# Norm sums, token scales and high parts between dense stages, attention by head pairs, and expert outputs by feature

## The reference, cut to what matters

```python
def rms(x):
    return x * lax.rsqrt(jnp.mean(x * x, axis=-1, keepdims=True) + EPS)

def modulate(h, shift, scale):
    return h * (1 + scale) + shift

def layer(x, xc, ...):                       # x and xc go through the same steps
    x = x + 0.5 * g1 * swiglu(modulate(rms(x), sh1, sc1), pre_wi, pre_wo)
    x = x + g2 * mixer(modulate(rms(x), sh2, sc2), ...)
    x = x + 0.5 * g3 * swiglu(modulate(rms(x), sh3, sc3), post_wi, post_wo)

def window_gqa(...):                         # 16 query heads, 4 key heads, head width 64
    # scores of 128 queries over 256 latent and 256 context keys, masked beyond 128 tokens
    p = jax.nn.softmax(jnp.concatenate([s_w, s_c, sink_b], axis=-1), axis=-1)
    o = p_w @ v_w + p_c @ v_c

def peer_ffn(z, wq, subkeys, u_tab, v_tab):  # 8 heads x 16 experts for each token
    # expert, gate: the 16 best of 16 x 16 sums of two sub-key scores, and their softmax
    h = jnp.einsum('thkd,td->thk', u_tab[expert], zb)
    act = gate * jax.nn.gelu(h, approximate=False)
    return jnp.einsum('thk,thkd->td', act, v_tab[expert])
```

## Time and profile before

| | us |
|---|---|
| median of three executions | 4268.56 |
| lowest, highest | 4261.12, 4279.62 |
| the profiled execution | 4257.62 |
| its span, first to last instruction | 4255.8 |
| granted TensorE clock, mean | 0.978 of 2.4 GHz |

### The profile page before, as it was taken

How to read it: one execution, slowest core, us unless ns; L and a number is a source line. 1 busy time by engine, 2 the same in 40 slices (tenths; PEclk the granted TensorE clock), 3 DMA queues, 4 the chain that set the end, 5 groups by cost and what they waited for, 6 DMA issues and landing times. The chain is left out here.

```text
span 4255.8 us, 50533 instructions
## 1 busy us (share of the span) xinstructions
PE 3832.7 (90%) x17626; PEld 2701.9 (63%) x17626; DVE 2633.9 (62%) x5211; ACT 1667.1 (39%) x3644; POOL 624.1 (15%) x665
## 2 busy tenths in 40 slices
PE   6999988999999999998999888788789998887877
PEld 4788765788788865897878744233278787442322
DVE  6877556677565546656347666777553466677774
ACT  3222535323332245543225444444332254444443
POOL 1100000000000000000000143444300002444442
PEclk9999998999999999999999999999999999999999
DMA  5554111355333310553033599999920346999997
GB/s 213 202 184 173 70 40 55 119 181 171 128 141 131 125 61 1 199 186 120 11 129 129 220 420 420 420 420 420 375 80 21 129 146 248 420 420 420 420 420 310
DMA packets 135007, 904.29 MB, mean 212 GB/s; under 512 B 14855, under 2 KB 15879, under 8 KB 35168
## 3 DMA queue, kind: packets, MB, share of 16 engines
q0 software_dynamic: 95552, 620.97, 36.2%
q1 hardware_dynamic: 39200, 280.08, 18.5%
HBM read 899.90 MB, written 5.28 MB: 213 GB/s over the span
## 5 line engine op out<-in xcount | busy, mean ns | idle before, releaser
L2511 PE MATMUL ps<-arena 128*128 128x512 f32 x1640 | 809.8, 622 | 183.1 <-ACT arena L2574 181.5
L2670 DVE CUSTOM_DVE_ANT_0 arena<-arena 128x1024 f32<-128x1024 f32 x410 | 502.5, 1226 | 326.6 <-DMA arena<-peer_uv,arena 325.5
L620 DVE TENSOR_TENSOR w_lo<-wt,w_hi 128x1024 fp32r<-128x1024 f32 x388 | 475.4, 1225 | 351.7 <-ACT w_hi L602 328.1
L2511 PEld LDWEIGHTS ps<-arena 128*128 128x128 f32 x1640 | 292.4, 193 | 628.4 <-ACT arena L2574 402.0
L655 PE MATMUL ps<-h_hi,w_hi 128*128 128x512 f32 (+1 forms) x1744 | 649.4, 372 | 32.5 <-DVE h_lo L742 22.5
L2642 POOL DMA_INDIRECT arena<-peer_uv,arena x410 | 433.4, 1057 | 1583.3 <-DVEq L2633 989.2
L602 ACT ACTIVATE w_hi<-wt 128x1024 fp32r<-128x1024 f32 x388 | 407.6, 1058 | 636.1 <-PE ps L655 607.0
L655 PE MATMUL ps<-h_lo,w_hi 128*128 128x512 f32 (+1 forms) x1744 | 639.5, 367 | 0.0
L655 PE MATMUL ps<-h_hi,w_lo 128*128 128x512 f32 (+1 forms) x1744 | 639.2, 367 | 0.0
L450 PE MATMUL ps<-hT,wt 128*128 128x256 f32 x1632 | 407.0, 387 | 6.1 <-ACT hT L1389 5.1
L655 PEld LDWEIGHTS ps<-h_hi,w_hi 128*128 128x128 f32 x1744 | 332.1, 190 | 94.0 <-issue 17.7
(11 more groups left out here) (342 smaller groups left out, 5453.8 us busy)
## 6 DMA issues: line engine op xcount, KB each, us to landing
wt<-wstream SPq DMA_DIRECT2D x262, 1024.0 KB, 4.9
ada_t<-adastream POOLq DMA_DIRECT2D x133, 512.0 KB, 3.7
arena<-peer_uv,arena POOLq DMA_INDIRECT x410, 20.3
arena<-adastream POOLq DMA_DIRECT2D x11, 512.0 KB, 26.6
bias_by_query<-bias_by_distance POOLq DMA_DIRECT2D x1, 4096.0 KB, 17.3
arena<-bias_by_query POOLq DMA_DIRECT2D x1, 3072.0 KB, 12.1
xT<-tokens SPq DMA_DIRECT2D x1, 2048.0 KB, 15.2
cst<-consts SPq DMA_DIRECT2D x1, 1816.0 KB, 9.0
```

The source lines that it names most:

```text
L620: self.step(self.dve.tensor_tensor(lo, raw_group(g), hi.bitcast(F32), ALU.subtract))
L2511: ins = pe.matmul(bank, diag[n % DIAGS], row[:, at:at + 512], start=s == 0, stop=s == SLOTS - 1)
L2670: dve.tensor_tensor_reduce(u, u, ztok[:, t], 1.0, 0.0, ALU.mult, ALU.add, hbuf[:, t, s:s + 1]).then_inc(dot_ready.sem, 1)
```

## The change

1. **Norm sums by column.** `dve_part` adds into `rstd` (or, in `merge`, into the slot it used before) instead of `hT[:, 0]`, so that the squares' slots come free one by one. Residual m of a last pass now stands behind sum m-1, and not before it.
2. **Scale kept in the tokens.** Behind sum m-1 DVE writes `xT` times the next norm's scale into `hT` (`dve_scaled`, 2 instructions of 256 tokens for a chunk), for chunks 0 to 6; chunk 7 is done in the norm. The norm then multiplies `hT` by `rstd`.
3. **High parts written directly and used first.** ACT adds the shift and writes `h_hi` in one step (2 instructions instead of 3); DVE makes `h_lo` from `hT`, shift and `h_hi` (2 instead of 1). `pe_by_chunk` starts a chunk when `h_hi` is there: hi x hi and lo x hi for all columns, then waits for `h_lo` and adds hi x lo for all. The first FFN keeps its own norm but uses the new order on PE.
4. **`keep_on`** leaves the start of dense stages: 4 such products now stand right behind `pe_parts`, and in `b_out` they wait for one bank instead of four.
5. **Plain norms** (`ln1`, `lnf`): DVE multiplies by gain and `rstd` in one step; ACT's step is gone.
6. **Head pairs.** `b_attend` has 16 units of two heads: scores of two heads in two halves of the rows, 1024-wide maxima and copies, value products of the two heads alternating between column halves, two pairs of score banks and one pair of transpose banks.
7. **Experts by feature.** A slot makes eight products of 128 columns: a block of 128 features of the row is the stationary operand, `diag` the moving one, and the result has features on partitions. ACT's copies and PE's transposes at the end go.

```diff
-        def pe_parts(pe, mm, T):
+        def pe_parts(pe, mm, T, idle=0):
             pe.wait_ge(A_.free, A_.given_back())
             bank = A_.claim()
             pe.wait_ge(sum_ready.sem, sum_ready.due(pe))
-            mm(bank[:, 0:T], ones, hT[:, 0, 0:T], True, False)
+            mm(bank[:, 0:T], ones, rstd[:, 0:T], True, False)
             pe.wait_ge(part_ready.sem, part_ready.due(pe, DC))
             mm(bank[:, 0:T], ones, hT[:, DC - 1, 0:T], False, True, A_.full)
+            if idle:
+                pe.wait_ge(D_.free, D_.given_back())
+                keep_on(pe, D_.coming(), idle)
...
+            if last and m >= 2:
+                dve_part(dve, step, m - 1, T)
+            if last and nxt and m >= 2:
+                for k in (0, 1) if m == 2 else (m - 1,):
+                    dve_scaled(dve, step, k, T, *nxt)
+            dve.wait_ge(D_.full, D_.filled())
+            bank = D_.take()
...
+        def pe_by_chunk(pe, SW, columns, T, key):
+            for k in range(DC):
+                pe.wait_ge(h_hi_ready.sem, h_hi_ready.due(pe))
+                ws = []
+                for c, r, bank in columns:
+                    hi, lo = SW.next(*key(k, c))
+                    ws.append(hi)
+                    SW.mm(bank[:, 0:T], ((hi, h_hi[:, k, 0:T]), (lo, h_hi[:, k, 0:T])), k == 0, False, None)
+                pe.wait_ge(h_ready.sem, h_ready.due(pe))
+                for hi, (c, r, bank) in zip(ws, columns):
+                    SW.mm(bank[:, 0:T], ((hi, h_lo[:, k, 0:T]),), False, k == DC - 1, r.full if k == DC - 1 else None)
...
+                    for x in range(2):
+                        mm(s[:, x, :], qB[r, u, q * P:(q + 1) * P], kD[r, u // 2, :], True, False)
+                    for x in range(2):
+                        mm(s[:, x, far], ident, const("window", q, TOK)[:, far], False, True, SB.scored if x else None)
...
+                        for x in range(2):
+                            mm(o[x * HD:(x + 1) * HD, 0:P], vB[:, j, g * HD:(g + 1) * HD], t[:, x, j, :], j == 0, j == 3,
+                               SB.valued if j == 3 and x else None)
...
-                    for bank, at in zip(y_banks(t), (D, D + 512)):
-                        ins = pe.matmul(bank, diag[n % DIAGS], row[:, at:at + 512], start=s == 0, stop=s == SLOTS - 1)
+                    for m in range(DC):
+                        ins = pe.matmul(y_banks(t)[m // 4][:, (m % 4) * P:(m % 4 + 1) * P], row[:, D + m * P:D + (m + 1) * P],
+                                        diag[n % DIAGS], start=s == 0 and m % 4 == 0, stop=s == SLOTS - 1,
+                                        skip_group_check=True)
```

More of the change, by code:

```diff
@@ L523, in act_squares, with dve_norm @@
             act_parts(act, step, T)
[L525 to L530, removed]
+        def dve_norm(dve, T, gain, first):
             dve.wait_ge(rstd_ready.sem, rstd_ready.due(dve))
             for k in range(DC):
[L533 to L539, removed]
+                dve.scalar_tensor_tensor(out=hT[:, k, 0:T], in0=xT[:, k, 0:T], scalar=v(gain, first + k),
+                                         in1=rstd[:, 0:T], op0=ALU.mult, op1=ALU.mult).then_inc(h_ready.sem, 1)
         def modulate(act, l, which, T, k):
@@ L654, in mm @@
                 for i, (a, b) in enumerate(pairs):
[L655 removed]
+                    ins = self.pe.matmul(o, a, b, start=start and i == 0, stop=stop and i == len(pairs) - 1)
                 if inc is not None:
@@ L675, in h_parts, with pe_split_project @@
             return h_hi[:, k, t0:t1], h_lo[:, k, t0:t1]
-        def pe_split_project(pe, SW, name, cols, T, r, abreast=0, idle=0):
+        def pe_by_chunk(pe, SW, columns, T, key):
[9 more added lines that the diff above has]
+                    SW.mm(bank[:, 0:T], ((hi, h_lo[:, k, 0:T]),), False, k == DC - 1, r.full if k == DC - 1 else None)
+        def pe_split_project(pe, SW, name, cols, T, r, abreast=0):
             if abreast:
                 pe.wait_ge(r.free, r.given_back(abreast))
[L681 to L687, removed]
+                pe_by_chunk(pe, SW, [(c, r, r.claim()) for c in cols[:abreast]], T, lambda k, c: (name, 0, k * P, c))
             for c in cols[abreast:]:
@@ L808, in pe_ffn @@
                 pe.wait_ge(r.free, r.given_back(ABREAST))
-            abreast = [(half, j, r, r.claim()) for j in range(ABREAST) for half, r in ((0, A_), (1, D_))]
-            if not first:
-                keep_on(pe, abreast[-1][3], 7 if T == TOK else 5)
-            for k in range(DC):
-                pe.wait_ge(h_ready.sem, h_ready.due(pe))
-                for half, j, r, bank in abreast:
-                    w = SW.next(f"ffn_{which}_wi", l, k * P, half * FF + j * P)
-                    SW.mm(bank[:, 0:T], three(w, h_parts(k, 0, T)), k == 0, k == DC - 1,
-                          r.full if k == DC - 1 else None)
+            abreast = [(half * FF + j * P, r, r.claim()) for j in range(ABREAST) for half, r in ((0, A_), (1, D_))]
+            pe_by_chunk(pe, SW, abreast, T, lambda k, c: (f"ffn_{which}_wi", l, k * P, c))
             for part in range(0, FC, HALF):
@@ L1217, in dve_a_out @@
                 weights.ahead()
-                dve.wait_ge(D_.full, D_.filled())
-                dve_residual(dve, step, D_.take(), m, 0, 1, TOK, True)
+                dve_residual(dve, step, m, 0, 1, TOK, True, (0, 2))
         MB = Carve(SPLIT_END)
```

233 lines of the change are left out of this document (120 added, 113 removed).

## The result

| | before | after |
|---|---|---|
| median, us | 4267.68 (4 runs) | 4228.09 (4 runs) |
| lowest, highest | 4261.12, 4279.62 | 4219.72, 4229.76 |
| span of the profiled execution | 4255.8 | 4217.9 |

The ratio is 0.9899, with a 95% interval from 0.9877 to 0.9921: 39.6 us off the median, where 56 were forecast (4212). The time lies in the forecast range, which was 43 us wide. Measured again beside three experiments the same kernel gave 4232.63 us (6 runs), ratio 0.9904 (0.9881 to 0.9928).

A forecast was written before the change was run, and what follows sets the result against it. Gathers bound `peer`; PE bounds `b_attend` and the dense stages, with losses between these. Terms summed to -56 us: profiled 4257.6 to 4201.6, plus 11 for the median, 4212 us; eight-in-ten range 4190 to 4233.

The forecast's parts named there:

- the signs that the prediction set itself: Profile checks: first products 6.5 us behind the last stage, `b_attend` near 62 us; wrong if passages are still 9 us.
- Head pairs, -33: `b_attend`: 16 pairs at 3.62 us plus 4 us of filling make 62 us against 94.8.
- The rival that DVE takes the stage: `b_attend`: DVE sets the pace at 4.2 us a pair, +9 us, 4221 us in all; chance 0.14.
- `a_out` to `post 0`, -5.2: Dense passage: same sequence as `post 0` to `pre 1`, with no blocks or weights beside it on DVE; 5.2 us less.
- `post 0` to `pre 1`, -4.9: Dense passage: earlier sums and `rstd`, first product near 1131.3 instead of 1136.4; residual 7 late by up to 0.2 us.
- the 1 us forecast for the first norm: First norm: high products of chunk 6 run before PE's wait for its low part; -1 us, from 0 to -3.5.
- `b_out` to `post 1`, +0.7: 256-token passage: DVE's late scalings cost +3.8, earlier sums and fewer constants give back; +0.7 us, between -1.5 and +3.
- `pre 0` to `a_qkv` and `pre 1` to `b_qkv`: Passages with their blocks: earlier `rstd` gives 1.65 and 1.25 us, the norm's pace 1.85 each; -3.5 and -3.1 together.
- Plain norms, -2.6: ACT's step leaves the way: -1.6 us at the first `rwkv_in`, -0.7 at the second, -0.3 at the final norm.
- Experts by feature, -3.6: `peer`: slots stay below the gathers' pace; each of two stages ends 1.8 us earlier, -3.6 us.
- rival (c): `peer`: loads and products don't overlap, PE becomes the bound at 4.5 us a slot; +970 us, 5180 us; chance 0.03.
- Rival (b): Four dense passages: late residual 7 or a falling clock shrinks their 16.7 us gain to 6; 4222 us; chance 0.11.

The follow-up runs named there:

- the two best versions: Changed kernel with last chunk column by column, later scaling in `a_out`, `b_out` and for chunk 6: 4212.47 us; also without constants behind `pre 1` and `b_out`: 4198.03 us.

## Why the prediction came out as it did

The time came into the range, but not for the reasons given. The pairs came as worked out. The dense stages, forecast to give 17 us, gave next to nothing in all, and the range was wide enough to hold that. By the signs that the prediction set itself, one passage is wrong: counted as there, from the end of the last product, first products stand 7.5 to 8.8 us behind in three of the four passages of 512 tokens, where 6.5 was forecast, and 10.1 us behind in `a_out` to `post 0`, where 9 was called wrong. PE was busy 94.9% of `b_attend` (over 95% forecast) and DVE idle 0.73 us a pair (under 0.4), so DVE was further from the bound than I had it.

- **Head pairs, -33: right, -31.6.** Every term of a pair was read from rows of the kernel before, most of them of other stages, and stood within 0.02 us. The filling was 63.2 - 16 x 3.59 = 5.8 us instead of 4; 0.8 of it is the stretch at 1.2 GHz, the other 1 us is open. The rival that DVE takes the stage is out: DVE is busy 72% of it. The section PSUM Bottleneck of the Trainium skill's page "TensorEngine Tiling (Array Packing)" warns of this bound; in this stage it wasn't met. The pairs also left `b_out` 1.7 us longer, at a clock of 0.91 (the run with pairs alone), which wasn't forecast.
- **`a_out` to `post 0`, -5.2: wrong step, -1.2.** I wrote that DVE has "no blocks or weights beside it". It splits weights for each chunk there, 1.23 us. Four of the eight banks come full together, 22.5 us before the last product ends; the seven steps from residual 0 to residual 7, 4.09 us each in the middle, take 26.0 us. Without the added scalings the passage is 6.66 us: -5.0, nearly the size forecast. Its sums also ran partly at 1.2 GHz behind the longer waits (the row of 2.07 us above), which came in with the late residual.
- **`post 0` to `pre 1`, -4.9: right mechanism, -3.8.** The residual was 1.3 us late and not 0.2.
- **Abreast block: not in the sum, +8.1 in three bodies and +1.5 in `a_out` and `b_out`.** I looked at when PE may begin a chunk, and not at when a bank is full, for which `silu` and the next weight split wait. This term was missing in `post 0`, `pre 1` and `post 1`, and ate the 1 us forecast for the first norm as well.
- **`b_out` to `post 1`, +0.7: +1.6, and the body +0.6.** DVE's lateness was forecast. The constants were counted at -1.3; in truth they stand ahead of the stage's end for all engines, and the passage is 2.9 us shorter without them. The same at `pre 1` to `b_qkv` is 1.9 us.
- **`pre 0` to `a_qkv` and `pre 1` to `b_qkv`: -3.6 and -2.7, with nothing from their blocks.** The sums of about -3.5 and -3.1 came out, the split of them didn't: the passages alone were to give 1.65 and 1.25 us. In `pre 0` to `a_qkv` the sums behind the shorter wait ran at 2.4 GHz (1.10 and 1.13 us for the halves). This is luck in part: in three of the nine profiles with parts 1 to 3 the clock fell to 1.2 GHz for 3.4 us in this passage, and it took 9.2 us and not 8.0.
- **Plain norms, -2.6: -4.9 with the clock.** With the old norms before it the first `rwkv_in` gained nothing (65.1), nor did it in two of the runs with the last chunk by columns (65.1), all at the clock of 0.95 that it had before. In the second, 0.5 to 2.2 us were gained: 64.4 before at a clock of 0.97, then 62.2 to 62.5 at 0.98 to 1.00, and 63.8 and 63.9 at 0.96 and 0.97 in the two best versions. So at like clock the part is worth 0.1 to 0.5 us, near the 0.7 forecast at the second and not at the first.
- **Experts by feature, -3.6: -4.8** by the run without it. The 128-column rows kept their distance, 0.11 us, and rival (c) is out.
- **`rwkv_core`: not in the sum, +5.9 at the first.** It is the same program at a lower clock, in three profiles of three. The medians are 39.6 us apart in both measurements and the rest 43.6; this loss is of a size to explain that, but only the profiled executions show it.
- A reading: the DMA row of the page has eleven slices at nine tenths, and not twelve. Nothing hangs on it.

Rival (b), passages that give back their gain, is nearest to what happened, though through another wait: of 16.7 us forecast for four passages 11.3 came and the bodies took 9.6.

## What to carry to other kernels

Ask of every reordering not only when its first instruction may start but also when its last output is complete, and what stands in a program behind the engine that waits for it. A filler in front of a barrier is paid by all engines. Where a part of a program has a clock that moves its time by 13 us, compare stage by stage, and profile one kernel twice before you call such a part chance: of two stages here one was, and the other came out the same three times.

## What was not expected of the hardware

Two executions of the same kernel agreed in most stages within 0.1 us, and yet one stage took 99.3 and 112.4 us, by the granted clock alone (0.94 and 0.79). The same stage in the layer before took 105.09 to 105.11 us in three profiles, with its low stretches at the same places. Over the twelve profiled executions the two cores together took from 198.8 to 217.5 us.

A busy PE didn't bring the clock back at once: the single heads stayed at 1.2 GHz for 23.9 us, in which PE was busy 10.00 of each 10.00 us, and lost 11 us; the pairs in the same place had 3.4 us of it and lost 0.8. What decides it in either stage stays open.
